# Moving the modulation pieces between the stages of a two-block transformer, and one wait of TensorE ahead of the value stage

## The chip, the cores and the metric

The kernel runs on one core of one Trainium2 chip. The metric is the device time of one execution in microseconds (us); lower is better. Engines are named as in the profile: PE is TensorE (PEld its weight loads), DVE is VectorE, ACT is ScalarE, POOL is GpSimd and SP is SyncE, whose queue issues the weight stream.

## The reference

One sequence of 256 positions and 1024 features goes through two blocks of two layers each, in float32. The first block has attention of several kinds, cross attention to a memory, and a gated feed-forward part with a short convolution. The second block is modulated by a condition vector:

```
def ada_params(cond, w, b):
    return jnp.split(jax.nn.silu(cond) @ w + b, 6, axis=-1)
...
    for i in range(DEPTH):
        sh1, sc1, g1, sh2, sc2, g2 = [t[:, None, :] for t in ada_params(c, ada_w[i], ada_b[i])]
        ax = modulate(rms_norm_2(hx, norm_mix[i]), sh1, sc1)
        ...
        hx = hx + g1 * yx
        fx = modulate(rms_norm_2(hx, norm_ffn[i]), sh2, sc2)
        hx = hx + g2 * swiglu(fx, ffn_w1[i], ffn_w3[i], ffn_w2[i])
```

`yx` is the retention mixer's output in layer 0 and the convolution mixer's in layer 1. A context sequence enters layer 0 with its own shift and scale, from `ada_params(c_ctx, ...)`. `ada_params` needs the 1024 x 6144 matrix `ada_w` of each layer: 48 pieces of 128 output columns a layer, 96 in all. The condition is one vector, so each piece is a matrix-vector product. They don't depend on the activations, so they can be done anywhere ahead of their use.

## The kernel before

**Stages and the stream.** `STAGES` lists 26 stages in the order in which they run: name, layer, number of weight pieces, and how many modulation pieces ("ada") go with each step. A step is two weight pieces. For layer 0 and 1 of the first block the stages are `qkv` (11 steps), `mkv` (2), `out` (4), `mq` (1), `mo` (1), `up` (22) and `down` (11); then come the stages of the second block: `rq`, `rg`, `rk`, `rv`, `ro` (queries, gates, keys, values, output of the retention mixer), `f13` and `f2` (feed-forward), `cx`, `cb`, `co` (convolution mixer), `f13` and `f2`. Every piece, of either kind, is 128x1024 float32 (512 KB) and comes from one tensor, `stream_d`, in the order in which it is consumed. `stage_table` works out the places. Stages named in `INTO_X` carry no modulation piece in their last step.

**Ring.** SP copies piece after piece into `ring`, eight slots. Piece r is asked for once the counter `consumed` has reached r-7, and the counter `loaded` is raised for a piece when the piece five places later has been asked for. So a late consumer holds up later loads.

**A weight piece.** ACT copies it to `WH` (rounded to fp32r, L471), DVE makes the remainder `WL` = piece - `WH` (L981, raises `consumed`), and PE does 24 matmuls with it: 16 with `WH` (against the high and low half of the activations), then 8 with `WL`. `WH` and `WL` have two slots, so ACT and DVE prepare the piece after the next while PE works.

**A modulation piece** (`ada_piece`, L990 to L999) costs PE and ACT nothing: DVE multiplies the piece with the broadcast condition `crow` and accumulates the row sums into a column of `mod` (L998). For the first 16 of the 96 a second such instruction with `crow_ctx` fills `modc` (L996). In a step with one modulation piece DVE does it after the second `WL`, ahead of the stage's own extra work (`aside`). In the last step of a stage outside `INTO_X` it comes first. Step 0 of a stage that follows a "raw" norm has an order of its own (`late`): `WL`, both evacuations, `WL`, modulation piece.

**The qkv stage.** DVE evacuates each product into `P` with the row norm (`mixed`, L1323 and L1326) and raises `bank_free`; PE waits for that count before it writes the bank again. After steps 2 to 10 `aside(step)` follows, with the rotary turns (`sine` L1236, `turned_by` L1243), the memory norm (`memory_scaled`, L1120) and, at the end of `aside(4)`, `prod` (L1275), for which PE waits in `gate_sums`. POOL does `compressed_rows` (L1600, four instructions a call) and `cosine` (L1609) beside it.

**Modulations.** `modulations(part)` adds the bias to its part of `mod` (L1379) and makes the gains `gs` (L1389), one chained DVE instruction each. Part 0 stands at the start of the second block, part 1 after the value stage, part 2 ahead of the residual at the end of `f2` (its argument `ahead`). ACT waits for `mod_ready` in `raw_norm`.

**The value stage.** PE accumulates in `accs`. After piece 2 `ret_scores(0)` writes the banks `proj`, which ACT frees when it has evacuated the last keys (L910).

Of the kernel before, what the change touches and what calls it, by code (L numbers as in the profile page):

```python
# [9 lines left out]
KB = D // 128  # L10
# [23 lines left out]

STAGES = [("qkv", 0, 2 * MIX, 0), ("mkv", 0, 4, 1), ("out", 0, 8, 1), ("mq", 0, 2, 0), ("mo", 0, 2, 0),
          ("up", 0, 2 * FB, 0), ("down", 0, FB, 1),
          ("qkv", 1, 2 * MIX, 0), ("mkv", 1, 4, 1), ("out", 1, 8, 1), ("mq", 1, 2, 0), ("mo", 1, 2, 0),
          ("up", 1, 2 * FB, 0), ("down", 1, FB, 2),
          ("rq", 0, 8, 0), ("rg", 0, 16, 0), ("rk", 0, 8, 1), ("rv", 0, 16, 2), ("ro", 0, 16, 2),
          ("f13", 0, 2 * FB, 1), ("f2", 0, FB, 0),  # L40
          ("cx", 1, 16, 0), ("cb", 1, 8, 0), ("co", 1, 8, 0), ("f13", 1, 2 * FB, 0), ("f2", 1, FB, 0)]
INTO_X = ("out", "mo", "down", "ro", "f2", "co")
N_MOD = 48
# [159 lines left out]
def transformer(nc, xT_d, memT_d, ctxT_d, cond_d, stream_d, vecs_d, const_d, rope1_d, rope2_d, decay_d,  # L203
# [5 lines left out]
    with ctx:  # L209
# [190 lines left out]
        def mod_of(layer, c):  # L400
            return mod[:, 48 * layer + KB * c:48 * layer + KB * c + KB]
# [62 lines left out]
        def _(act):  # L464
# [370 lines left out]
            def second_ffn(k, layer):  # L835

                def swiglu(step, s):
                    if s == 0:
                        if is_first(step):
                            act.preload_act_table(ACT.Silu)  # L840
                        act.wait_ge(bank_free[0], step + (n["q"] + 2))
                        A(cv[:, 0, :], cv[:, 0, :], ACT.Silu, bias=cvs[:, 0, S:S + 1]).then_inc(silu_ready, 1)  # L842
                    else:
                        upper(step, step + (n["pair"] + 1))
                weights(k, swiglu, peel=2, late=raw_root)
                n["pair"] += FB
                if layer == 0:
                    raw_norm(k + 1, gs[:, 2, :], 0, 1, shift=mod_of(1, 0), ready=3)
                else:
                    weights(k + 1, tail=squares(1))  # L850
                    n["x"] += 8
# [93 lines left out]
            def last_head(step):  # L945
                if step == 0:
                    ret_root(RET_HEADS - 1)
                if step == 1:
                    ret_high(RET_HEADS - 1)
            raw_norm(K + 4, gs[:, 1, :], 0, 1, shift=mod_of(0, 3), ready=2, after=last_head)  # L950
            second_ffn(K + 5, 0)

            def conv_in(i, s):
# [20 lines left out]
        def _(dve):  # L974
# [42 lines left out]
            def weights(k, evac=None, per=0, peel=False, before=None, gate=None, into_x=False, after=None, raw=None, ahead=None, late=None):  # L1017
# [3 lines left out]
                def part(i, last):  # L1021
# [33 lines left out]
                    for s in range(2):  # L1055
# [6 lines left out]
                        if late and evac and s == 1 and type(i) is int and i == 1:  # L1062
                            split(next_piece(st, i, s), st["p0"] + 5, s)
                            evac(1, 0)
                            dve.wait_ge(mm_done, st["p0"] + 4)
                            before(i, s)
                            evac(1, 1)
                            if st["ada"]:
                                ada(0)
                            continue  # L1070
                        if before:
                            dve.wait_ge(mm_done, i * 2 + (st["p0"] + s + 1))
# [304 lines left out]
            def biased(j0, j1):  # L1377

                chain.link(V.tensor_tensor(mod[:, j0:j1], mod[:, j0:j1], vecs[:, V_ADAB + j0:V_ADAB + j1], ALU.add))  # L1379

            def modulations(part):

                dve.wait_ge(consumed, TABLE[K + (0, 4, 7)[part]]["r0"])
                biased((0, 16, 48)[part], (16, 48, 96)[part])
                scales = [[(0, mod_of(0, 1), V_MIX2), (4, modc[:, 8:16], V_MIX2)],
                          [(1, mod_of(0, 4), V_FFN2)],
                          [(2, mod_of(1, 1), V_MIX2 + KB), (3, mod_of(1, 4), V_FFN2 + KB)]][part]
                for c, scale, gain in scales:
                    chain.link(V.scalar_tensor_tensor(out=gs[:, c, :], in0=scale, scalar=1.0, in1=vecs[:, gain:gain + KB],  # L1389
                                                      op0=ALU.add, op1=ALU.mult))  # L1390
                dve.sem_inc(mod_ready, 1)
# [15 lines left out]
            def second_ffn(k, layer):  # L1407
# [15 lines left out]
                n["pair"] += FB  # L1423
                n["silu"] += FB
                if layer == 0:
                    weights(k + 1, gate=mod_of(layer, 5), into_x=True, raw=(gs[:, 2, :], 0, mod_of(1, 0)), ahead=lambda: modulations(2))
                else:
                    weights(k + 1, gate=mod_of(layer, 5), into_x=True)

# [95 lines left out]
                if part == 1 and h:  # L1525
                    ret_low(h - 1)
            weights(K + 3, heads, before=values, after=lambda step: None)
            modulations(1)

            def last_head(step):  # L1530
                if step == 0:
# [126 lines left out]
        def _(pe):  # L1658
# [449 lines left out]

            def ret_scores(h):
                if h == 0:  # L2110
                    for s in range(2):
                        pe.wait_ge(bank_free[s], n["q"] + 1)
                    pe.wait_ge(rope_done, 4 * DEPTH + 8)
                else:
                    pe.wait_ge(ret_w, 2 * h)
                if h >= 2:
                    pe.wait_ge(ret_rms, h - 1)
                for jt in range(4):
                    for c in range(2):
                        ins = mm(proj[jt // 2][:, jt % 2 * S:jt % 2 * S + S], K2[:, 2 * h + c, 128 * jt:128 * jt + 128], Q2[:, 2 * h + c, :],  # L2120
                                 c == 0 and jt % 2 == 0, c == 1)
                ins.then_inc(ret_sc, 1)
# [17 lines left out]
                ins.then_inc(ret_ms, 1)  # L2140

            st = TABLE[K + 3]
            for p in range(16):
                h, part = divmod(p, 4)
                s = p % 2
# [146 lines left out]
```

## Time and profile before

| | |
|---|---|
| median of 3 runs | 1614.93 us (1614.89 to 1616.33) |
| profiled execution | 1614.93 us; span of its trace 1613.2 us |
| PE busy | 1573.2 us, 98% of the span |
| DVE busy | 1161.8 us, 72% |
| ACT busy | 818.5 us, 51% |
| POOL busy | 86.1 us, 5% |
| data read | 291.4 MB, 181 GB/s over the span |

A busy PE is one that has a matmul under way; matmuls are pipelined. Times in rows are microseconds from the start of the span.

### The profile page before, as it was taken

What the parts mean: (1) busy time and instruction counts of PE and PEld (TensorE: products, weight loads), DVE (VectorE), ACT (ScalarE), POOL (GpSimd) and SP (SyncE); (2) the same over time, 40 slices, a digit from 0 to 9 for tenths busy, and PEclk for the clock granted to TensorE, in tenths of its full rate; (3) what the DMA queues carried; (4) which work ended last, traced back from release to release, by engine and by line L of the source; (5) the groups of instructions that cost most, each with busy time, mean ns of one, the idle gap of its engine ahead of it and who ended that gap; (6) DMA issues with size and microseconds to landing.
All of it is one profiled execution on the core that took longest, in us unless ns stands there. A gap on an engine that the chain in (4) does not pass through costs nothing. (4 is left out here: it accounts for less than half of the span.)

```text
span 1613.2 us, 35961 instructions
## 1 busy us (share of the span) xinstructions
PE 1573.2 (98%) x12298; PEld 1463.1 (91%) x12298; DVE 1161.8 (72%) x1781; ACT 818.5 (51%) x1343; POOL 86.1 (5%) x91
## 2 busy tenths in 40 slices
PE   8999899999999989999999999999999999999998
PEld 7977789999997869999989888889999999999997
DVE  5884789988877478998867445568988468677644
ACT  5555666653556576664555212235555355555533
POOL 2100001110300001110000100000000000000000
PEclk9999999999999999999999999999999999999999
DMA  9530435458743235557945543358888545455551
GB/s 361 190 132 14 157 131 173 176 187 275 270 146 131 77 133 181 172 180 272 340 128 186 164 137 128 133 190 297 272 277 276 199 163 184 162 185 181 183 182 50
DMA packets 84234, 297.45 MB, mean 184 GB/s; under 512 B 9664, under 2 KB 12480, under 8 KB 83392
## 3 DMA queue, kind: packets, MB, share of 16 engines
q1 hardware_dynamic: 78912, 283.24, 51.0%
q10 hardware_dynamic: 5248, 13.18, 2.4%
q8 instruction: 52, 0.85, 0.2%
q14 instruction: 22, 0.18, 0.0%
HBM read 291.40 MB, written 1.05 MB: 181 GB/s over the span
## 5 line engine op out<-in xcount | busy, mean ns | idle before, releaser
L981 DVE TENSOR_TENSOR WL<-ring,WH 128x1024 fp32r<-128x1024 f32 x427 | 524.7, 1230 | 260.3 <-ACT WH L471 259.0
L471 ACT ACTIVATE WH<-ring 128x1024 fp32r (+1 forms) x419 | 441.6, 1057 | 517.8 <-PE projs L1663 249.0
L1663 PE MATMUL projs<-AH,WH 128*128 128x256 f32 (+2 forms) x2120 | 538.1, 291 | 8.9 <-ACT WH L471 4.1
L1663 PE MATMUL projs<-AL,WH 128*128 128x256 f32 (+2 forms) x2120 | 530.9, 287 | 0.3
L1663 PEld LDWEIGHTS projs<-AH,WH 128*128 128x128 f32 x2120 | 399.2, 189 | 23.7 <-DVE mk L1346 7.7
L1663 PEld LDWEIGHTS projs<-AL,WH 128*128 128x128 f32 x2120 | 401.2, 190 | 5.3 <-DVE AL L1141 1.7
L1663 PE MATMUL projs<-AH,WL 128*128 128x256 f32 (+2 forms) x2192 | 315.2, 285 | 0.2 <-DVE WL L981 0.2
L1663 PEld LDWEIGHTS projs<-AH,WL 128*128 128x128 f32 x2192 | 285.2, 189 | 7.5 <-DVE WL L981 2.5
L1663 PE MATMUL accs<-FH,WH 128*128 (+1 forms) x768 | 190.5, 284 | 2.0 <-ACT WH L471 2.0
L1663 PE MATMUL accs<-FL,WH 128*128 (+1 forms) x768 | 189.7, 281 | 0.0
L1663 PEld LDWEIGHTS accs<-FH,WH 128*128 128x128 f32 x768 | 144.3, 188 | 3.3 <-issue 3.3
L1663 PEld LDWEIGHTS accs<-FL,WH 128*128 128x128 f32 x768 | 144.8, 189 | 0.0
L998 DVE SCALAR_TENSOR_TENSOR ring<-ring,crow 128x1024 f32 (+1 forms) x96 | 118.3, 1232 | 2.9 <-DVE G L1489 0.7
L1663 PE MATMUL accs<-FH,WL 128*128 (+1 forms) x768 | 113.4, 282 | 0.0
L814 ACT ACTIVATE cv<-mk,vecs 128x256 f32<-128x256 f32 x88 | 53.1, 603 | 97.7 <-DVE mk L1346 97.7
L1663 PEld LDWEIGHTS accs<-FH,WL 128*128 128x128 f32 x768 | 101.1, 188 | 0.0
L1663 PE MATMUL accs<-AH,WH 128*128 128x256 f32 (+2 forms) x272 | 68.5, 286 | 3.4 <-DVE AL L1197 1.9
L1663 PE MATMUL accs<-AL,WH 128*128 128x256 f32 (+2 forms) x272 | 67.2, 281 | 0.0
L1355 DVE SCALAR_TENSOR_TENSOR cv<-mk,vecs,cv 128x254 f32<-128x254 f32 x88 | 53.6, 609 | 11.5 <-DVE cv L1353 0.3
L1663 PEld LDWEIGHTS accs<-AH,WH 128*128 128x128 f32 x272 | 51.2, 188 | 6.5 <-DVE AL L1197 3.1
L1638 POOL TENSOR_TENSOR FL<-prod,FH 128x256 f32 x44 | 36.2, 824 | 364.8 <-ACT FH L535 364.8
L1663 PE MATMUL accs<-WH,AH 128*128 128x512 f32 x128 | 51.7, 404 | 0.0
(261 smaller groups left out, 1867.2 us busy)
## 6 DMA issues: line engine op xcount, KB each, us to landing
ring<-in_stream SPq DMA_DIRECT2D x532, 512.0 KB, 3.8
W1v<-in_w ACTq DMA_DIRECT2D x2, 1024.0 KB, 7.2
W1k<-in_w ACTq DMA_DIRECT2D x2, 1024.0 KB, 10.3
D<-in_decay ACTq DMA_DIRECT2D x4, 512.0 KB, 5.0
x<-in_xT SPq DMA_DIRECT2D x2, 512.0 KB, 5.3
memT<-in_memT SPq DMA_DIRECT2D x1, 1024.0 KB, 11.3
mq<-P ACTq DMA_DIRECT2D x8, 128.0 KB, 5.9
ctxT<-in_ctxT ACTq DMA_DIRECT2D x1, 1024.0 KB, 8.1
```

The source lines that it names most:

```text
L471: A(WH[:, s, :], ring[:, r % RING, :], ACT.Copy).then_inc(wh_ready, 1)
L814: A(cv[:, s, :], us[:, s, :], ACT.Identity, bias=cb, scale=w2).then_inc(tap_ready, 1)
L981: V.tensor_tensor(WL[:, s, :], ring[:, r % RING, :], WH[:, s, :].bitcast(F32), ALU.subtract).then_inc(consumed, 1)
L998: V.scalar_tensor_tensor(out=piece, in0=piece, scalar=1.0, in1=crow[:], op0=ALU.mult, op1=ALU.mult, accum_out=mod[:, bass.ds(j, 1)]).then_ ...
L1355: V.scalar_tensor_tensor(out=cv[:, s, 2:S], in0=us[:, s, 0:S - 2], scalar=vecs[:, bass.ds(j + cw, 1)], in1=cv[:, s, 2:S], op0=ALU.mult, op ...
L1638: G.tensor_tensor(FL[:, bass.ds(step, 1), :].squeeze(1), prod[:], FH[:, bass.ds(step, 1), :].squeeze(1).bitcast(F32), ALU.subtract).then_i ...
L1663: return T.matmul(out, lhsT, rhs, start=start, stop=stop, skip_group_check=True)
```

## The change

The modulation pieces are handed out differently over the stages; their sum stays 96. `qkv` of layer 1 gets 1 a step (11 pieces, was 0), `out` of layer 1 gets 0 (was 3), `rk` gets 2 a step (8, was 4), `f13` of the second block's layer 0 gets 0 (was 22), its `f2` gets 1 a step (10, was 0). After the change all 48 pieces of layer 0 are done ahead of the second block, so `modulations` has two parts in place of three. And the wait for the two `proj` banks moves from `ret_scores(0)` to the head of the value stage.

```
 STAGES = [
...
-          ("qkv", 1, 2 * MIX, 0), ("mkv", 1, 4, 1), ("out", 1, 8, 1), ("mq", 1, 2, 0), ("mo", 1, 2, 0),
+          ("qkv", 1, 2 * MIX, 1), ("mkv", 1, 4, 1), ("out", 1, 8, 0), ("mq", 1, 2, 0), ("mo", 1, 2, 0),
           ("up", 1, 2 * FB, 0), ("down", 1, FB, 2),
-          ("rq", 0, 8, 0), ("rg", 0, 16, 0), ("rk", 0, 8, 1), ("rv", 0, 16, 2), ("ro", 0, 16, 2),
-          ("f13", 0, 2 * FB, 1), ("f2", 0, FB, 0),
+          ("rq", 0, 8, 0), ("rg", 0, 16, 0), ("rk", 0, 8, 2), ("rv", 0, 16, 2), ("ro", 0, 16, 2),
+          ("f13", 0, 2 * FB, 0), ("f2", 0, FB, 1),
...
-                    raw_norm(k + 1, gs[:, 2, :], 0, 1, shift=mod_of(1, 0), ready=3)
+                    raw_norm(k + 1, gs[:, 2, :], 0, 1, shift=mod_of(1, 0), ready=2)
...
-            raw_norm(K + 4, gs[:, 1, :], 0, 1, shift=mod_of(0, 3), ready=2, after=last_head)
+            raw_norm(K + 4, gs[:, 1, :], 0, 1, shift=mod_of(0, 3), after=last_head)
...
                             evac(1, 1)
-                            if st["ada"]:
-                                ada(0)
                             continue
...
-            def modulations(part):
-
-                dve.wait_ge(consumed, TABLE[K + (0, 4, 7)[part]]["r0"])
-                biased((0, 16, 48)[part], (16, 48, 96)[part])
-                scales = [[(0, mod_of(0, 1), V_MIX2), (4, modc[:, 8:16], V_MIX2)],
-                          [(1, mod_of(0, 4), V_FFN2)],
-                          [(2, mod_of(1, 1), V_MIX2 + KB), (3, mod_of(1, 4), V_FFN2 + KB)]][part]
+            def modulations(layer):
+
+                dve.wait_ge(consumed, TABLE[K + (0, 7)[layer]]["r0"])
+                biased(48 * layer, 48 * layer + 48)
+                scales = [(2 * layer, mod_of(layer, 1), V_MIX2 + KB * layer), (2 * layer + 1, mod_of(layer, 4), V_FFN2 + KB * layer)]
+                if layer == 0:
+                    scales.append((4, modc[:, 8:16], V_MIX2))
                 for c, scale, gain in scales:
...
-                    weights(k + 1, gate=mod_of(layer, 5), into_x=True, raw=(gs[:, 2, :], 0, mod_of(1, 0)), ahead=lambda: modulations(2))
+                    weights(k + 1, gate=mod_of(layer, 5), into_x=True, raw=(gs[:, 2, :], 0, mod_of(1, 0)), ahead=lambda: modulations(1))
...
             weights(K + 3, heads, before=values, after=lambda step: None)
-            modulations(1)
...
             def ret_scores(h):
                 if h == 0:
-                    for s in range(2):
-                        pe.wait_ge(bank_free[s], n["q"] + 1)
                     pe.wait_ge(rope_done, 4 * DEPTH + 8)
...
             st = TABLE[K + 3]
+            for s in range(2):
+                pe.wait_ge(bank_free[s], n["q"] + 1)
             for p in range(16):
```

## Rows read from the trace of the kernel before

**Rows 1.** Windows: busy of PE, PEld, DVE, ACT, POOL (count), clock, DMA, GB/s.
```profile
420.00:430.00 10.00, 10.00 (x87) 10.00 (x86) 7.25 (x9) 3.77 (x4) 4.61 (x4) 1.00 0.96 371
```
**Rows 2.** Chain of work that ended last: start, length, what.
```profile
1247.19 63.61 PE accs L1663 x528
...
1414.10 0.02 ACT rms L577
...
1536.98 63.59 PE accs L1663 x528
```
**Rows 3.** Timeline of ACT at the start of f13, layer 0.
```profile
1124.01 0.47 ACT L577 ACTIVATE rms<-ob,const 128x256 f32<-128x256 f32 x1 [0.79 <-PE ob L1663]
```
**Rows 4.** Who waited for whom, PE, 415 to 500 us: total, times, longest.
```profile
PE ob L1663 <- DVE prod L1275: 0.7, 1, 0.7
```
**Rows 5.** The ring with crow, ns min/median/max; then rows_v.
```profile
L998 DVE SCALAR_TENSOR_TENSOR ring<-ring,crow x96: 1215/1220/2317, 98.4 to 1245.8; 128x1024 f32 x55, 128x1024 f32<-128x1024 f32 x41
...
L1600 POOL TENSOR_TENSOR rows_v<-P,vecs x8: 710/1154/1643, 23.4 to 424.3; 64x240 f32<-64x240 f32 x8
```
**Rows 6.** Timeline around the longest modulation piece, POOL and DVE.
```profile
938.22 2.30 POOL L1646 TENSOR_TENSOR K<-K,rope 128x512 f32<-128x512 f32 x1 [8.96 <-DMA mq<-K]
939.29 2.32 DVE L998 SCALAR_TENSOR_TENSOR ring<-ring,crow 128x1024 f32<-128x1024 f32 x1
```
**Rows 7.** Timeline of POOL, DVE and ACT, steps 0 and 1 of qkv, layer 1.
```profile
420.35 4.68 POOL L1600 TENSOR_TENSOR rows_v<-P,vecs 64x240 f32<-64x240 f32 x4 [70.83 <-DVE P L1326]
421.32 0.42 DVE L1326 TENSOR_TENSOR P<-accs,rstd 128x256 f32<-128x256 f32 x1
422.01 1.75 DVE L981 TENSOR_TENSOR WL<-ring,WH 128x1024 fp32r<-128x1024 f32 x1 [0.28 <-ACT WH L471]
423.75 1.06 ACT L471 ACTIVATE WH<-ring 128x1024 fp32r<-128x1024 f32 x1 [1.77 <-PE accs L1663]
426.58 1.06 ACT L471 ACTIVATE WH<-ring 128x1024 fp32r<-128x1024 f32 x1 [1.77 <-PE projs L1663]
```
**Rows 8.** Timeline of DVE and POOL, steps 3 to 5 of that stage.
```profile
438.22 4.29 POOL L1600 TENSOR_TENSOR rows_k<-P,vecs 64x240 f32<-64x240 f32 x4 [2.50 <-DVE P L1243]
440.75 0.43 DVE L1326 TENSOR_TENSOR P<-projs,rstd 128x256 f32<-128x256 f32 x1 [0.27 <-PE projs L1663]
441.84 1.75 DVE L981 TENSOR_TENSOR WL<-ring,WH 128x1024 fp32r<-128x1024 f32 x1 [0.67 <-ACT WH L471]
442.59 3.86 POOL L1609 TENSOR_TENSOR P<-P,rope 128x512 f32<-128x512 f32 x2
447.83 0.42 DVE L1275 TENSOR_TENSOR prod<-ob,rstd 128x256 f32<-128x256 f32 x1
```
**Rows 9.** Timeline where keys end and values begin, ACT and PE.
```profile
932.33 0.58 ACT L910 ACTIVATE K<-projs 128x512 f32<-128x512 f32 x1
931.17 0.39 PE L1663 MATMUL accs<-WH,AH 128*128 128x512 f32 x1
```
**Rows 10.** Timeline at the ends of out and mo, layer 1.
```profile
568.99 0.59 PE L1663 MATMUL ob<-still 128*128 128x512 bf16 x2
576.88 1.75 DVE L1114 RECIPROCAL rstd<-rms 128x256 f32<-128x256 f32 x1 [1.75 <-ACT rms L577]
599.16 0.59 PE L1663 MATMUL ob<-still 128*128 128x512 bf16 x2
606.43 1.75 DVE L1114 RECIPROCAL rstd<-rms 128x256 f32<-128x256 f32 x1 [1.14 <-ACT rms L577]
```
**Rows 11.** Timeline of DVE at the start of the second block.
```profile
803.84 0.17 DVE L1389 SCALAR_TENSOR_TENSOR gs<-mod,vecs 128x8 f32<-128x8 f32 x1
804.04 0.17 DVE L1389 SCALAR_TENSOR_TENSOR gs<-modc,vecs 128x8 f32<-128x8 f32 x1
```
**Rows 12.** Timeline of DVE at the end of f2, layer 0.
```profile
1307.55 0.21 DVE L1379 TENSOR_TENSOR mod<-mod,vecs 128x48 f32<-128x48 f32 x1
1308.67 3.23 DVE L1012 SCALAR_TENSOR_TENSOR x<-accs,mod,x 128x256 f32<-128x256 f32 x8 [0.50 <-PE accs L1663]
```

## The prediction

> **What bounds the kernel now.** I read the page's busy times, then the chain that ended last, the waits of PE, and the timelines of the stages that the change touches. PE has 1573 of 1613 us busy, so only two things cost time: work that PE has to do, and moments at which PE stands still. The change gives PE no work and takes none away. A modulation piece is DVE work of 1.22 us [rows 5] (1.15 from one start to the next), and it matters only where DVE already sets PE's pace. So I ask of each stage whether DVE is late there.
>
> PE needs 2.83 us for a weight piece in qkv: ACT, which waits for the end of each, starts at 423.75 and at 426.58 and takes 1.06 us [rows 7]. Then comes DVE's `WL` (1.15), so DVE is ready some 2.3 us after a piece ended. PE wants that `WL` one piece and 16 of 24 matmuls later, 2.83 + 1.9 = 4.7 us after. DVE may be about 2.4 us late before PE notices. One extra piece of 1.15 us is hidden in a plain step; it shows where DVE has much else to do.
>
> **f13, layer 0: 22 pieces leave.** The row norm's root starts at 1124.01 [rows 3] and PE gets to f2 at 1247.19: 123.18 us. The same stage of layer 1, with no modulation piece, takes 1536.98 - 1414.10 = 122.88 us [rows 2]. So 22 pieces, 25 us of DVE work, cost PE 0.30 us today. Gain: 0.3.
>
> **f2, layer 0: 10 pieces come.** Both f2 stages run 63.6 us [rows 2] and the steps have room (2 x 1.15 + 1.15 of 5.76 us). What changes is the end. Today DVE begins `modulations` at 1307.55, and after it still waits 0.50 us for PE before the residual at 1308.67 [rows 12]. Afterwards the last modulation piece fills 1307.5 to 1308.65, and `modulations` follows it (0.25 for the bias add, 0.20 for each of two `gs`, from start to start as in [rows 11]): the residual starts 0.65 to 0.7 us late. Behind it are queued the low halves, for which PE waits. Loss: 0.7.
>
> **qkv, layer 1, step 0.** Here the piece is number 15 of the first 16, so it is two chained instructions. DVE would start them at 421.35, where it now evacuates step 1 [rows 7]. POOL runs its four `rows_v` instructions then, 0.71 us each when undisturbed [rows 5]. How do the two get along? A POOL instruction that runs from 938.22 to 940.5 and a modulation piece that starts at 939.29 meet: the piece takes 2.32 us and not the median 1.22 [rows 5, 6], that is, 1.1 from POOL's end on. The `WL` at 422.01 takes 1.75 us in the middle of `rows_v` [rows 7]. So I take it that each of the two waits until the other's instruction has ended. (The Trainium skill, SBUF — State Buffer, section "SBUF: two separate sides", says the same: the port pair is an exclusive lock, held for the whole instruction, against a DVE instruction with two SBUF inputs. By that rule, the trace agrees: the 2.32 us. If instead the two only ran side by side, this term would be near zero and the next 1.3.)
> Alternating: first instruction 421.99 to 423.15, POOL to 423.9, second to 425.1, POOL to 425.8 (meanwhile the evacuation from `accs`, which isn't held up in rows 7), `WL` of step 2 from 425.8 to 427.0. PE starts step 2 at 423.75, where ACT was released [rows 7], and wants that `WL` at 425.65. Loss 1.4; without the collisions DVE would have it at 425.35: 0. From above: both instructions at 2.32 us give 427.9 or so, 2.3. I take 1.4.
>
> **qkv, steps 3 and 4.** `prod` at 447.83 [rows 8] is already what PE waits for (0.7 us [rows 4]). Ahead of it DVE gets one modulation piece in step 3 and one in step 4, 2.3 us; its idle time on the way is 0.27 + 0.67 us [rows 8], which leaves 1.3 to 1.4. But POOL's six instructions (`rows_k`, two `cosine`) start when `turned_by(0)` is done, so they shift back by 1.1 too, and their end at 442.59 + 3.86 = 446.45 [rows 8] moves past DVE's `sine(2)`. In the same alternation, times without the 1.4 of before: the piece of step 4 waits for the third `rows_k` (0.7), `turned_by(1)` for the fourth (0.6), `sine(2)` for a `cosine` (1.2), and `memory_scaled`, which runs free today, for the last `cosine` (1.2). `prod` is evacuated at about 450.8: late by 3.0. Ends: 1.3 and 3.5, the latter with one more short collision. I take 2.9, near the upper end, because today's `WL` at 441.84 shows this very alternation (1.75 us in the middle of `rows_k` [rows 8]).
>
> **qkv, end.** The piece of step 10 comes ahead of the evacuation that frees the bank for mkv. Following the steps with 1.15 more each, DVE catches up by step 9 (PE has 7 us of side work in steps 5 to 9), then `aside(9)` and two pieces in a row delay the evacuation of step 10 to 0.2 to 0.3 us after PE wants the bank. Loss 0.3 (0 to 0.5). Cover that may go: the stream now asks for three pieces a step while W1 and the swaps load, and the DMA share is already 0.96 from 420 to 430 us, at the full clock of 1.00 [rows 1]. The ring has five to six pieces in hand, about 10 us; I cost it at 0, bound 2.
>
> **mkv, layer 1.** The two-instruction piece is gone there, 1.2 us of DVE; what follows waits for ACT and PE. 0.
>
> **out, layer 1: 3 pieces leave.** From PE's first warm-up matmul to the reciprocal of the norm it is 576.88 - 568.99 = 7.89 us at the end of out, with a modulation piece in front, and 606.43 - 599.16 = 7.27 at the end of mo, without [rows 10]. Same norm, same shapes. Gain: 0.6.
>
> **Start of the second block.** `modulations` has one more chained instruction (0.20 from start to start) and a wider bias add, in front of the `gs` and the root on which everything waits [rows 11]. Loss: 0.2. The part that stood after rv, 0.4 us of DVE, was hidden; 0. The dropped `ready=2` waits for something long past; 0.
>
> **rk: 4 more pieces.** A keys piece has matmuls of 512 columns and keeps PE nearly twice 2.83 us, in which DVE has one `WL`, one modulation piece (2.3 us together) and part of a turn. 0.
>
> **The moved wait.** Today PE begins the values at 931.17, and ACT frees the second key bank at 932.33 + 0.58 = 932.91 [rows 9]; nobody minds, since the scores come only after the third piece. Afterwards PE stands until 932.95 or so before its first matmul. Behind it is all of rv, and the list of PE's waits from 930 to 1118 us is empty, so nothing takes it up. Loss: 1.8 (1.6 to 1.9).
>
> **Sum.** -0.3 + 0.7 + 1.4 + 2.9 + 0.3 - 0.6 + 0.2 + 1.8 = +6.4 us. The profiled execution's own time was 1614.93 (span 1613.2 and 1.7 around it), which is also the median, so 1621.3 us, 0.4% slower. All bounds at their low end: -0.3 + 0.6 + 0 + 1.3 + 0 - 0.6 + 0.2 + 1.6 = +2.8, 1617.7. All at the high end: -0.3 + 0.7 + 2.3 + 3.5 + 0.5 - 0.6 + 0.2 + 1.9 + 2 = +10.2, 1625.1.
>
> **Rivals.**
> *Collisions with POOL don't add up.* The qkv stage loses just its 1.3 to 1.6. For it: of 96 modulation pieces the median took 1.22 us [rows 5]. Against it: the long `WL`s [rows 7, 8]. With 0 and 1.4 for the two terms the sum is +3.5, 1618.4: at the edge of what can be told. Chance 0.2.
> *The stream falls behind in qkv.* Three pieces a step, 277 GB/s, plus 2 MB of W1 against some 400 GB/s; ACT would wait for `loaded`. It needs 1.4 MB to queue up in the 10 us that the ring covers. Against it: down of layer 0 runs at three pieces a step, and PE waits for ACT once there, 1.0 us. 2 MB at 400 GB/s are 5 us of stream; if half of that reaches PE, the total is +9, 1624, and all of it gives 1626.5. Chance 0.1.
> *Faster: f13 gives more than 0.3.* If PE in f13 were held back in every step by DVE, 22 steps would have to give 0.45 us each to outweigh 6.7 us of losses and reach 0.2%. Place: the steady steps; deciding point 0.45 us a step. Against it: 0.3 us over the stage [rows 2, 3]. 1611.7 at that point. Chance 0.03.
> *The moved wait is free*, if PE stood anyway for `WH` of the first values. Against it: PE starts at 931.17 [rows 9]. Then 1619.5. Chance 0.07.
> The forecast itself: 0.6.
>
> **Chances.** 0.2% is 3.2 us, about what a measurement of this kernel can tell from no change. Slower by more: the forecast, the stream, the free wait, and two fifths of the first rival (the rest of it within), 0.85; within: 0.12; faster: 0.03. The range runs from the first rival's low edge to short of the second's.
>
> **What would show it.** In the profile after: PE waits on DVE's `WL` near 425 us (1.4), and on `prod` (3 to 4 us in place of 0.7); modulation pieces of over 2 us in qkv; a hole of 1.8 us ahead of the first values; 122.9 us for f13; the residual of f2 without a wait for PE. I am wrong if PE's wait for `prod` stays under 2 us or ACT waits for the stream in qkv.

## The result, and the profile after

| | before | after |
|---|---|---|
| median, same chip | 1615.08 us (1614.89 to 1616.33) | 1626.86 us (1625.55 to 1627.89) |
| profiled execution | 1614.93 us, span 1613.2 | 1627.96 us, span 1626.3 |
| DVE busy | 1161.8 us | 1166.5 us |

The ratio is 1.0076, with a 95% interval from 1.0063 to 1.0088. The change costs 11.8 us in the medians and 13.0 us between the two profiled executions. The forecast was +6.4 us, so the sign was right and the size was about half of what came. The range was to end short of the stream rival's 1624 us, and even the sum of all upper bounds, 1625.1 us, lies below the measured time. Lines of the kernel after stand two or three lower than before in places: `prod` is L1273, `mixed` L1321 and L1324, `mk` of the up stage L1344, PE's matmul helper L1660.

First, who PE waited for in the qkv and mkv stages (415 to 500 us; total, times, longest):

```profile
PE ob L1660 <- DVE prod L1273: 2.8, 1, 2.8
PE projs L1660 <- DVE WL L981: 0.9, 1, 0.9
PE projs L1660 <- DVE P L1324: 0.5, 1, 0.5
PE accs L1660 <- ACT WH L471: 0.2, 1, 0.2
```

The wait for `prod` has grown from 0.7 us [rows 4] to 2.8. The other two new waits are those forecast near 425 us (0.9 for `WL`, where 1.4 stood) and at the end of the stage. The forecast had put the wait for `prod` at 3 to 4 us. The timeline of steps 0 and 1, DVE, POOL and ACT:

```profile
420.25 6.64 POOL L1597 TENSOR_TENSOR rows_v<-P,vecs 64x240 f32<-64x240 f32 x4 [70.84 <-DVE P L1324]
421.21 1.75 DVE L996 SCALAR_TENSOR_TENSOR cprod<-ring,crow_ctx 128x1024 f32<-128x1024 f32 x1
...
423.01 1.62 DVE L998 SCALAR_TENSOR_TENSOR ring<-ring,crow 128x1024 f32<-128x1024 f32 x1
...
424.90 1.41 DVE L981 TENSOR_TENSOR WL<-ring,WH 128x1024 fp32r<-128x1024 f32 x1
...
427.62 1.07 ACT L471 ACTIVATE WH<-ring 128x1024 fp32r<-128x1024 f32 x1 [2.92 <-PE projs L1660]
```

POOL's four `rows_v` take 6.64 us beside the two products, where they took 4.68 [rows 7]; the products take 1.75 and 1.62 us and not 1.22 [rows 5]. The `WH` that marks the end of a PE piece comes at 427.62, 1.04 later than at 426.58 [rows 7]. Steps 3 to 5, and the work after `prod`:

```profile
440.40 5.29 POOL L1597 TENSOR_TENSOR rows_k<-P,vecs 64x240 f32<-64x240 f32 x4 [3.40 <-DVE P L1241]
...
445.04 1.74 DVE L998 SCALAR_TENSOR_TENSOR ring<-ring,crow 128x1024 f32<-128x1024 f32 x1
445.77 3.83 POOL L1606 TENSOR_TENSOR P<-P,rope 128x512 f32<-128x512 f32 x2
...
446.71 1.76 DVE L1241 TENSOR_TENSOR P<-P,cv 128x512 f32<-128x512 f32 x1
448.51 1.65 DVE L1234 TENSOR_TENSOR cv<-swapped,rope 128x512 f32<-128x512 f32 x1
...
450.99 0.42 DVE L1273 TENSOR_TENSOR prod<-ob,rstd 128x256 f32<-128x256 f32 x1
...
455.57 0.28 ACT L739 ACTIVATE csum<-accs 128x128 f32<-128x128 f32 x1 [2.81 <-PE accs L1660]
```

`prod` comes 3.2 us later than at 447.83 [rows 8], after three DVE instructions in a row that take longer beside POOL. Two of the three did so in the kernel before as well:

```profile
443.52 1.78 DVE L1243 TENSOR_TENSOR P<-P,cv 128x512 f32<-128x512 f32 x1
445.33 1.67 DVE L1236 TENSOR_TENSOR cv<-swapped,rope 128x512 f32<-128x512 f32 x1
```

New is the modulation piece ahead of them, at 1.74 us. But the partial sums, evacuated as `csum`, are late by still more: 4.58 us after `prod` began, where the kernel before needed 3.10 (447.83 to 450.93). The windows say why (busy of PE, PEld, DVE, ACT, POOL, then the granted clock, DMA share, GB/s):

```profile
420.00:430.00 10.00, 9.12 (x77) 8.91 (x76) 9.97 (x14) 3.19 (x3) 6.57 (x4) 1.00 0.98 392
430.00:440.00 10.00, 10.00 (x87) 10.00 (x86) 8.40 (x14) 4.24 (x4) 3.21 (x2) 1.00 1.01 386
450.00:460.00 10.00, 8.54 (x170) 8.39 (x171) 8.37 (x16) 3.17 (x6) 0.00 (x0) 0.83 0.48 168
```

and the last of these windows in the kernel before:

```profile
450.00:460.00 10.00, 10.00 (x140) 9.73 (x130) 7.51 (x14) 5.36 (x10) 0.00 (x0) 1.00 0.47 160
```

From 450 to 460 us the granted clock is 0.83: after its wait PE spent part of the stretch at the lower of its two levels (1.2 and 2.4 GHz). DMA is full from 420 to 440, yet ACT never waits for the stream there.

The largest part lies where nothing was changed, in `up` of layer 1. DVE in the kernel before, from one loop pass to the next:

```profile
679.88 0.42 DVE L1346 TENSOR_TENSOR mk<-projs,rstd 128x256 f32<-128x256 f32 x1
...
685.41 0.43 DVE L1362 TENSOR_TENSOR prod<-cv 128x256 f32<-128x256 f32 x1 [0.21 <-DVE cv L1355]
685.81 0.42 DVE L1346 TENSOR_TENSOR mk<-projs,rstd 128x256 f32<-128x256 f32 x1
```

and in the kernel after:

```profile
682.21 0.42 DVE L1344 TENSOR_TENSOR mk<-projs,rstd 128x256 f32<-128x256 f32 x1 [0.19 <-issue]
...
687.75 0.43 DVE L1360 TENSOR_TENSOR prod<-cv 128x256 f32<-128x256 f32 x1 [0.21 <-DVE cv L1353]
688.36 0.42 DVE L1344 TENSOR_TENSOR mk<-projs,rstd 128x256 f32<-128x256 f32 x1 [0.19 <-issue]
```

The same instructions take 5.93 us a pass before and 6.15 after. The 0.22 us are a gap ahead of the pass's first instruction that no wait explains ("issue"). From the first to the last of ACT's 22 L821, one a step, it is 123.72 and 127.94 us.

The moved wait, at the start of the values:

```profile
942.98 0.58 ACT L910 ACTIVATE K<-projs 128x512 f32<-128x512 f32 x1
...
943.66 0.47 PE L1660 MATMUL accs<-WH,AH 128*128 128x512 f32 x1 [1.68 <-issue]
```

PE now begins after ACT's last keys and not 1.2 us ahead of them [rows 9]. Then f13 of layer 0: the norm's root, and from the chain the last of f13 and the first of f2:

```profile
1136.47 0.48 ACT L577 ACTIVATE rms<-ob,const 128x256 f32<-128x256 f32 x1 [0.79 <-PE ob L1660]
...
1144.16 115.20 PE projs L1660 x960
1259.36 57.62 PE accs L1660 x480
```

That is 122.89 us, where it was 123.18. And the end of f2, layer 0:

```profile
1319.62 1.22 DVE L998 SCALAR_TENSOR_TENSOR ring<-ring,crow 128x1024 f32 x1
...
1321.65 2.44 DVE L1012 SCALAR_TENSOR_TENSOR x<-accs,mod,x 128x256 f32<-128x256 f32 x6 [0.16 <-PE accs L1660]
```

This view ends inside the residual, so it shows six of its eight instructions. The residual starts 12.98 us later than before [rows 12], but the matmuls of the last piece ahead of it only 12.18 (1307.67 and 1319.85): it is DVE that is late now, by 0.8 us, and the 0.16 us put down to PE are no wait for it.

All of it, stage by stage, from the times of ACT's instructions at the borders (after minus before):

| stretch | us | forecast |
|---|---|---|
| up to qkv, layer 1 | -0.1 | 0 |
| qkv and mkv, `prod` to `csum` at its old 3.10 us | +4.0 | +4.6 |
| the 1.48 us more between `prod` and `csum` | +1.5 | none |
| attention of layer 1 | +1.2 | none |
| out | -0.6 | -0.6 |
| up | +4.2 | none |
| start of the second block | +0.2 | +0.2 |
| rq, rg, rk | +0.2 | 0 |
| start of the values | +1.9 | +1.8 |
| f13, layer 0 | -0.3 | -0.3 |
| f2, layer 0 | +0.8 | +0.7 |
| sum | +13.0 | +6.4 |

### The profile page after: what moved, and what is told of

It reads as the page before. It is cut to its first block, busy times and chain, and to the rows that moved or that the text cites. A ratio compares the mean times of both kernels' runs of the same rounds, so it can differ in the third digit from the quotient of the medians.

```text
span 1626.3 us, 35908 instructions
## 1 busy us (share of the span) xinstructions
PE 1576.1 (97%) x12283; PEld 1466.4 (90%) x12298; DVE 1166.5 (72%) x1780; ACT 816.6 (50%) x1343; POOL 87.6 (5%) x91
## 4 chain that ended last, share of the span: by engine, by line
PE 72%; DVE 14%; ACT 7%; issue 5%; DVEq 1%; ACTq 1%; DMA 0%; SPq 0%; POOL 0%
PE projs L1660 34%; PE accs L1660 32%; PE ob L1660 5%; DVE WL L981 4%; ACT WH L471 3%; DVE mk L1344 2%; DVE cv L1353 2%; DVE cv L1351 1%; ACT FH L535 1%; DVE rstd L1112 1%; ACT AH L562 1%; PE projs L1906 1%; ACT scr L641 1%; DVE ring L998 1%; DVE prod L1360 0%
## 5 line engine op out<-in xcount | busy, mean ns | idle before, releaser
L1660 PE MATMUL projs<-AH,WH 128*128 128x256 f32 (+2 forms) x2120 | 538.5, 291 | 12.5 <-ACT WH L471 4.3
L1660 PE MATMUL projs<-AL,WH 128*128 128x256 f32 (+2 forms) x2120 | 530.9, 287 | 0.3
L1660 PEld LDWEIGHTS projs<-AH,WH 128*128 128x128 f32 x2120 | 399.5, 189 | 28.9 <-DVE mk L1344 14.0
L1660 PEld LDWEIGHTS projs<-AL,WH 128*128 128x128 f32 x2120 | 401.1, 189 | 5.5 <-DVE AL L1139 1.7
L1660 PE MATMUL projs<-AH,WL 128*128 128x256 f32 (+2 forms) x2192 | 315.3, 286 | 1.2 <-DVE WL L981 1.2
L1660 PEld LDWEIGHTS projs<-AH,WL 128*128 128x128 f32 x2192 | 285.2, 189 | 8.7 <-DVE WL L981 4.1
L1660 PE MATMUL accs<-FH,WH 128*128 (+1 forms) x768 | 190.4, 284 | 2.0 <-ACT WH L471 2.0
L1660 PE MATMUL accs<-FL,WH 128*128 (+1 forms) x768 | 189.6, 281 | 0.0
L1660 PEld LDWEIGHTS accs<-FH,WH 128*128 128x128 f32 x768 | 144.3, 188 | 3.3 <-issue 3.3
L1660 PEld LDWEIGHTS accs<-FL,WH 128*128 128x128 f32 x768 | 144.8, 189 | 0.0
L998 DVE SCALAR_TENSOR_TENSOR ring<-ring,crow 128x1024 f32<-128x1024 f32 (+1 forms) x96 | 120.3, 1253 | 2.8 <-DVE G L1487 0.7
L1660 PE MATMUL accs<-FH,WL 128*128 (+1 forms) x768 | 113.4, 282 | 0.0
L1660 PEld LDWEIGHTS accs<-FH,WL 128*128 128x128 f32 x768 | 101.0, 188 | 0.0
L1660 PE MATMUL accs<-AH,WH 128*128 128x256 f32 (+2 forms) x272 | 68.6, 286 | 3.4 <-DVE AL L1195 1.9
L1660 PE MATMUL accs<-AL,WH 128*128 128x256 f32 (+2 forms) x272 | 67.2, 281 | 0.0
L1660 PEld LDWEIGHTS accs<-AH,WH 128*128 128x128 f32 x272 | 51.2, 188 | 6.4 <-DVE AL L1195 3.1
L1660 PE MATMUL accs<-WH,AH 128*128 128x512 f32 x128 | 51.8, 405 | 1.7 <-issue 1.7
```

What stands on the lines that cost most here:

```text
L998: V.scalar_tensor_tensor(out=piece, in0=piece, scalar=1.0, in1=crow[:], op0=ALU.mult, op1=ALU.mult, accum_out=mod[:, bass.ds(j, 1)]).then_ ...
L1660: return T.matmul(out, lhsT, rhs, start=start, stop=stop, skip_group_check=True)
```

## The experiments

All are timed beside the kernel before on the same chip. "Prod" is when `prod` starts, counted from the root of the qkv norm of layer 1 (ACT's L577, 416.09 before and 415.98 after): 31.74 us before, 35.01 after. "Mkv end" is ACT's last `Vm` of that layer on the same scale: 80.98 and 86.48.

### The place of the up loop in VectorE's program

Five runs here, and two further down, move DVE's loops by instructions that do nothing. A wait on a semaphore long complete is put ahead of the memory attention, where DVE has time; the compiler joins two such waits into one instruction.

```diff
                 weights(k0 + 3, before=cross_q, late=root)
                 n["q"] += 1
+                for _ in range((a, b)[i]):
+                    dve.wait_ge(setup_v, 3)
                 attend(units_memory())
```

`(a, b)` are the waits in layer 0 and in layer 1. The first two runs have them in layer 1 alone, 33 in the kernel before (17 instructions) and 30 in the kernel after (15). The next three are the kernel before with (16, 38), (32, 32) and (64, 64).

> The kernel before, with 33 waits on a semaphore that is long complete, put on VectorE just ahead of the memory attention of layer 1; they become 17 instructions, so that VectorE's up loop of layer 1 stands at the place in its program that it has in the changed kernel. All computation is the same. Theory (the loop's place in the program sets what its jump back costs): the period of a step of that loop goes from 5.93 to 6.15 us and the time rises by about 4.4 us, to some 1619. Rival (the loop was slowed by its state on entry, its ring slots or the traffic, not by its place): the period stays 5.93 us and the time is within 1 us of the kernel before.

Measured: 1615.44 us against 1614.89, ratio 1.0004 (0.9994 to 1.0013). The step stays at 5.93 us. This went against the theory, in the form in which it stood.

> The changed kernel, with 30 such waits at the same place, 15 instructions, so that the up loop of layer 1 stands 32 instructions behind its place in the kernel before. Theory that place counts, with a period of 32 instructions or a divisor of it: the step goes back from 6.15 to 5.93 us and the time falls by 4.4 us to about 1622.5. If place counts with a longer period: the step has some third length between 5.9 and 6.2 us. Rival (not the place): 6.15 us stays, time within 1 us of the changed kernel.

Measured: 1624.41 us, ratio 1.0059 (1.0043 to 1.0076). The step is 6.03 us, between the two. The identical loop, in an otherwise identical kernel, goes 0.12 us faster a pass for 15 idle instructions that run once. And the gap has moved to another place of the pass, ahead of the second convolution instruction:

```profile
680.91 0.48 DVE L1354 SCALAR_TENSOR_TENSOR cv<-mk,vecs,cv 128x255 f32<-128x255 f32 x1
681.66 0.61 DVE L1356 SCALAR_TENSOR_TENSOR cv<-mk,vecs,cv 128x254 f32<-128x254 f32 x1 [0.27 <-DVE cv L1354]
...
684.28 0.49 DVE L1356 SCALAR_TENSOR_TENSOR cv<-mk,vecs,cv 128x254 f32<-128x254 f32 x1
```

So the place does count, and the first run had the wrong one. The trace shows what its count had left out: each modulation piece is two instructions on the chip, the product and a read of its sum.

```profile
445.04 1.74 DVE L998 SCALAR_TENSOR_TENSOR ring<-ring,crow 128x1024 f32<-128x1024 f32 x1
446.71 0.08 DVE L998 DVE_READ_ACCUMULATOR ring<-ring,crow 128x1 f32 x1
```

The qkv stage is written out step by step, so its 11 pieces, one of them double, put 12 such reads ahead of the loop, and less is left in mkv and out: 10 net, and the shift is 27, not 17. The instructions in the traces give the same: from the root to the loop the kernel after executes 298 on DVE and the kernel before 283, and of `out`'s loop, which is passed three times, a pass has 8 and 14. With each pass beyond the first taken off, 282 and 255 are left.

> The kernel before, with waits on a long complete semaphore on VectorE ahead of both memory attentions: 8 instructions in layer 0 and 19 in layer 1. The up loop of layer 1 then stands 27 instructions behind its place in the kernel before, which is its shift in the changed kernel too once the reads of the accumulator are counted (17 instructions of the program and some 10 such reads; the 17 of the first padded run left those out). Theory (place): layer 1's step is 6.15 us, up by 0.22, as in the changed kernel, so +4.4 us there; layer 0's step, now 8 instructions further, leaves 6.03 or not, by at most 0.1 to 0.2 us either way (2 to 4 us in all). Rival (not the place but what the changed kernel did ahead of the loop): layer 1 stays at 5.93 us.

Measured: 1619.97 us against 1614.93, ratio 1.0030 (1.0019 to 1.0042). Layer 1's step is 6.15 us, and the unexplained gap is there, in a kernel that has no part of the change:

```profile
681.78 0.42 DVE L1364 TENSOR_TENSOR prod<-cv 128x256 f32<-128x256 f32 x1 [0.21 <-DVE cv L1357]
682.40 0.42 DVE L1348 TENSOR_TENSOR mk<-projs,rstd 128x256 f32<-128x256 f32 x1 [0.19 <-issue]
```

Layer 0, moved by 8, stays at 6.03. That shows the place as the cause of the 4.2 us, and it was got by moving nothing else. Why a place costs time isn't shown.

> The same with 16 instructions in each layer: the up loop of layer 0 moves by 16 and that of layer 1 by 32. Theory that the cost goes by the place modulo 32 or a divisor: layer 1 stays at 5.93 us; if the period is 16, layer 0 stays at 6.03 too and the time is that of the kernel before plus at most 1 us; if it is 32, layer 0's step changes, by up to 0.2 us (4 us in all). Rival (only the absolute distance counts): layer 1's step changes too.

Measured: 1615.53 us, ratio 1.0003 (0.9993 to 1.0013). Layer 0 at +16 goes down to 5.91 us a step, layer 1 at +32 goes up to 6.04: no period of 16 or 32. The two cancel in the total, which alone would have read "no effect".

> As the run with 16 and 32 instructions of shift, with 32 and 64. If the cost of a place repeats every 64 instructions, layer 1's step is 5.93 us as in the kernel before; layer 0's, at +32, can't be told from the others. Rival (no such period, the shift counts in another unit than the program's instructions): another length between 5.90 and 6.15 us.

Measured: 1613.81 us, ratio 0.9992 (0.9982 to 1.0001). Layer 1 at +64 is at 5.93 again, layer 0 at +32 at 5.91. A period of 64 fits; one point doesn't prove it. Every run of this study, layer 1:

| shift | 0 | 17 | 25 | 27 | 32 | 42 | 64 |
|---|---|---|---|---|---|---|---|
| step, us | 5.93 | 5.93 | 5.90 | 6.15 | 6.04 | 6.03 | 5.93 |
| runs | before | 1 | 4 | 4 | 1 | 2 | 1 |

At 25 stand the two runs below that leave out a double or two single pieces, the one that puts the pieces behind, and the last run of this document; at 27 the kernel after, its two versions with only PE edits, and the padded kernel before.

### The qkv stage and TensorE's clock

Filler ahead of the gate sums, layer 1 only, in the kernel after:

```diff
                     if step == 5:
+                        if i == 1:
+                            turn_over(10, acc[1])
                         gate_sums()
```

> The changed kernel, with 10 matmuls 128x512 on zeros into a free bank ahead of the gate sums of qkv step 5 in layer 1 (about 2.1 us at 213 ns each, inside TensorE's wait of 2.8 us for prod). Theory (that wait lets TensorE's clock fall, and the narrow partial sums then run at the lower level): the granted clock of 450:460 goes from 0.83 to about 1.00, the stretch from the gates' exponential to the partial sums' eviction from 3.02 to about 1.0 us, and the time falls by about 2 us to 1625. Rival (the stretch is long for a data wait or for the count of columns): clock or not, it stays near 3 us and the time stays within 0.5 us, or rises by what of the filler isn't covered.

Measured: 1624.22 us, ratio 1.0054 (1.0037 to 1.0071). The window:

```profile
450.00:460.00 10.00, 9.31 (x188) 8.62 (x187) 9.26 (x16) 3.24 (x7) 0.00 (x0) 1.00 0.49 161
```

`prod` is as late as before (35.02), `csum` follows 3.09 us after it, mkv ends at 84.99 and not 86.48. The clock was the whole of the 1.5 us in that execution. Against this stands the padded kernel after, which has no filler and the same wait of 2.8 us, but a clock of 1.00. So I set all runs side by side:

| kernel | PE's wait for `prod` | clock 450:460 | `prod` to `csum` |
|---|---|---|---|
| before; five padded ones; after, pieces of steps 3 and 4 left out | 0.7 to 0.8 | 1.00 | 3.08 to 3.10 |
| after | 2.8 | 0.83 | 4.58 |
| after, 15 padded | 2.8 | 1.00 | 3.09 |
| after, wait back | 2.8 | 0.66 | 5.17 |
| after, piece of step 0 left out | 3.4 | 0.66 | 5.16 |
| after, filler (two kernels) | 0.7 | 1.00 | 3.09 |
| after, pieces behind | 1.3 | 1.00 | 3.08 |

A long wait makes the fall possible, not sure: it came in three profiled executions of four, with two sizes, and in none of the ten with a wait of 1.3 us or less. (The Trainium skill, TensorE: Matmul & The Clock Gate, section "HAM oscillation — how this bites in real kernels", has long waits of TensorE lower its clock for the matmuls behind them. The traces agree in kind: 0.83 and 0.66 behind waits of 2.8 and 3.4 us, though one wait of 2.8 us left it at 1.00.) All recorded executions point the same way, if by little: the mean granted clock over the whole kernel is 0.9952 to 0.9958 in the four kernels with the long wait, and 0.9965 to 0.9978 in the others. The kernel before took 1613.4 us in its executions at 0.999 and 1616.2 in those at 0.996, so between it (0.9975) and the kernel after (0.9958) the clock makes an estimated 1.6 us. The same view settles the 1.2 us of layer 1's attention, which the change doesn't touch. From ACT's last `WH` of mkv to its first of out it is 53.16 or 53.17 us in four profiles (before, and three changed kernels), all with 1.00 from 530 to 550 us; it is 54.28 to 54.36 in the ten others, all with a clock under 1 in that stretch (0.83 in 540:550 of the kernel after). Padded kernels before have it as well. So it goes with the execution and not with the change, and the profiled execution of before was one of the four. What lowers the clock there wasn't tried.

Two pieces left out of the kernel after, with their columns zeroed, so that the result of this kernel lacks them:

```diff
+                if leave_out:
+                    if ctx_too:
+                        chain.link(V.memset(modc[:, j:j + 1], 0.0))
+                    V.memset(mod[:, j:j + 1], 0.0).then_inc(consumed, 1)
+                    return
...
-                        ada_piece(ada_place(st, i, a, last), j, j < 16 if type(j) is int else st["j0"] < 16, last)
+                        ada_piece(ada_place(st, i, a, last), j, j < 16 if type(j) is int else st["j0"] < 16, last,
+                                  st["name"] == "qkv" and i in (3, 4))
```

> The changed kernel, whose modulation pieces of qkv steps 3 and 4 in layer 1 are left out: their two columns are set to zero in place of the products, their data is still loaded. Theory (these two pieces make prod late, 3.27 us with the step 0 share of 1.15): prod comes some 2.1 us earlier after the start of the stage, at about 32.9 us, TensorE's wait for it is 0.7 us and not 2.8, the granted clock of 450:460 is 1.00, and the memory stage ends 2.1 + 1.5 us earlier. Rival (the wait comes from the rotation's slow neighbours on GpSimd, or from the whole backlog since step 0): prod earlier by less than 1 us.

Measured: 1619.40 us, ratio 1.0025 (1.0016 to 1.0035). `prod` at 32.90 us, 2.1 earlier; wait 0.7; clock 1.00; mkv ends at 82.86, 3.6 earlier. As the theory had it. (The up loop, at +25, went down to 5.90 us too, which is why the total fell by more.)

The same with `i in (0,)`:

> The changed kernel, whose modulation piece of qkv step 0 in layer 1, with its context product, is left out in the same way. Theory (with both at 1.75 and 1.62 us beside GpSimd's compression rows they hold up the second lower half WL and with it the second step): the fifth of TensorE's pieces ends 1.15 us earlier, as in the kernel before (10.49 us after the stage's start, not 11.64), and the rest of the stage follows by as much, less what the waits of steps 3 and 4 take up. Rival (the 1.15 us are made up by the wait at prod anyway): the step is earlier, but prod is not.

Measured: 1621.88 us, ratio 1.0044 (1.0030 to 1.0058). The fifth piece is at 10.49 us, exactly as in the kernel before, so step 0's piece costs the stage 1.15 us at that point. But `prod` moves from 35.01 to 34.38 only, and PE waits 3.4 us for it:

```profile
PE ob L1666 <- DVE prod L1279: 3.4, 1, 3.4
PE projs L1666 <- DVE P L1330: 0.5, 1, 0.5
```

The rival is right in part: without step 0's piece `prod` is late by 2.6 (34.38 - 31.74), without those of steps 3 and 4 by 1.2 (32.90 - 31.74), with all of them by 3.3. They don't add up in full. The timelines between the pieces of steps 2 and 3 show where the half microsecond is. In this run POOL starts its `cosine` just ahead of a `WL`, which takes 2.32 us:

```profile
434.26 1.29 POOL L1612 TENSOR_TENSOR P<-P,rope 128x512 f32<-128x512 f32 x1 [0.61 <-DMA mq<-P]
434.31 2.32 DVE L981 TENSOR_TENSOR WL<-ring,WH 128x1024 fp32r<-128x1024 f32 x1
```

In the kernel after the `WL` comes first and takes 1.22:

```profile
434.63 1.22 DVE L981 TENSOR_TENSOR WL<-ring,WH 128x1024 fp32r<-128x1024 f32 x1
434.83 2.17 POOL L1606 TENSOR_TENSOR P<-P,rope 128x512 f32<-128x512 f32 x1 [3.64 <-DMA mq<-P]
```

From there on DVE is 0.6 us apart in the two runs, as `prod` is, and not 1.15.

Then the order of DVE's work in a step:

```diff
+                behind = st["name"] == "qkv" and st["ada"] == 1
...
-                        if st["ada"]:
+                        if st["ada"] and not behind:
                             ada(0)
...
-                        if not last and s >= 2 - st["ada"]:
+                        if not last and s >= 2 - st["ada"] and not behind:
                             ada(s - (2 - st["ada"]))
...
                         part(i, i + 1 == st["steps"])
                         after(i)
+                        if behind and i + 1 < st["steps"]:
+                            piece(i, 0, False)
```

> The changed kernel, with each modulation piece of qkv in layer 1 put behind the work of its step (rotation, scaling of the memory, gate product) on VectorE instead of ahead of it. Theory (prod waits because two pieces stand ahead of it in VectorE's order): the piece of step 4 is out of prod's way and that of step 0 comes a little later; prod comes 1.2 to 1.8 us earlier than in the changed kernel (35.0 us after the stage's start), TensorE's wait for it falls from 2.8 to 1.0-1.6 us, and the memory stage ends as much earlier, more if the clock stays at 1.00. Rival (the delay is only handed to the next step's lower halves): the end of the memory stage is within 0.5 us of the changed kernel at the same clock.

Measured: 1619.30 us, ratio 1.0029 (1.0020 to 1.0039). `prod` at 33.43, 1.6 us earlier; PE waits 1.3 us for it; mkv ends at 83.57. That is 1.4 us before the kernel with filler, which had the same clock of 1.00, and 2.9 before the kernel after.

```profile
PE ob L1667 <- DVE prod L1280: 1.3, 1, 1.3
...
PE projs L1667 <- DVE WL L981: 0.9, 1, 0.9
PE projs L1667 <- DVE P L1331: 0.7, 1, 0.7
```

All 96 pieces are done, in the same steps. The two orders differ by 7.6 us in their medians, taken in different sets of runs; the up loop, shifted to +25 by this edit, has 4.5 of it (127.94 and 123.39 us from the first to the last L821), the qkv stage 2.9.

### The moved wait, and three causes at once

The wait for the banks back in `ret_scores(0)`, in the kernel after:

```diff
             def ret_scores(h):
                 if h == 0:
+                    for s in range(2):
+                        pe.wait_ge(bank_free[s], n["q"] + 1)
                     pe.wait_ge(rope_done, 4 * DEPTH + 8)
...
-            for s in range(2):
-                pe.wait_ge(bank_free[s], n["q"] + 1)
             for p in range(16):
```

> The changed kernel, with the wait for the free banks ahead of the first retention scores again and not ahead of the first values. Theory (it costs the 1.81 us that the traces show between the last key and the ro norm): the time falls by 1.8 us to about 1625.0. Rival (the retention loop has slack of its own, so that it was something else in that stretch): within 0.5 us of the changed kernel.

Measured: 1625.47 us, ratio 1.0061 (1.0044 to 1.0078). From the last keys' evacuation to ACT's first `WH` of the values it is 4.63 us, as in the kernel before, against 6.52 in the kernel after: 1.89 us. In the medians, of different sets of runs, 1.4 of them show.

> The changed kernel with three of the causes taken back at once: the filler ahead of the gate sums, the wait for the free banks at its old place, and VectorE's 15 instructions ahead of layer 1's up loop (6.03 us a step). Theory (they add): 2.6 us from the loop, 1.9 us from the wait and the clock's 1.5 us in the profiled stretch, so about 1621 us; what is left over the kernel before is 4.0 us in the qkv and memory stages, 2.0 in the loop. Rival (they overlap or bring new waits): 1622.5 or more.

Measured: 1621.26 us, ratio 1.0042 (1.0027 to 1.0058), where 1621 was expected. The filler, the old wait and the 15 instructions add: clock 1.00, step 6.03 us, 84.97 at the end of mkv.

### Both up loops at faster places

> The kernel before, with waits on a long complete semaphore on VectorE ahead of the memory attentions: 16 instructions in layer 0 and 9 in layer 1, so that the up loop of layer 0 stands 16 and that of layer 1 25 instructions further. Theory (place): layer 0's step is 5.91 us as it was at +16 (6.03 before; 21 steps between the first and the last mark, so -2.3 us), layer 1's is about 5.90, as in the runs that left pieces out, which stood 2 accumulator reads ahead of the changed kernel's +27 (5.93 before; -0.6 us); together some 1612 us, 0.2% faster than the kernel before. Rival (the shift has to be right to the instruction, and mine is counted from the program, not from the chip's code): layer 1 at 5.93 to 6.15 us, time between 1612.5 and 1617.

Measured: 1613.44 us against 1614.90, ratio 0.9991 (0.9982 to 1.0000). It is the kernel before with 16 and 9 idle instructions, (32, 18) waits. Both loops went as forecast, 5.91 and 5.90 us a step, and the time didn't: it was put at 1612. In the profile the two loops give back 2.2 and 0.3 us. Of that 1.5 shows in the median: 0.1% faster than the kernel before, at the edge of what can be told, and 0.8% faster than the kernel after. It keeps the old places of the modulation pieces; none of the runs says that the new ones are worth having.

## Why the prediction was wrong

**The step that failed** is the rule on which the whole sum was built: "I ask of each stage whether DVE is late there", asked only of stages that get or lose a piece, so that an untouched one costs nothing. A loop of DVE that PE hangs on here also paid for where its instructions lie in the program. That was 4.2 us in `up`, shown by the padded kernels: the kernel before with the loop moved by the same 27 instructions has the 6.15 us step and takes 1620.0 us. Against that one the kernel after stands 6.9 us higher in the medians of different sets of runs (as ratios, 1.0076 less 1.0030 is 7.4 us, give or take some 2.7). The forecast of 6.4 was for that difference, without knowing it; that it comes so near is luck in part, since the 7 us hold a cost of the clock that the sum didn't have. No bound of the range held such a term, and none of the rivals did.

**The clock** was taken as full ("at the full clock of 1.00 [rows 1]"), though the sum itself let PE wait 3 to 4 us for `prod`. What follows such a wait ran at a lower clock in three profiled executions of four: 1.5 us in that of the kernel after, 0 to 2.1 in others.

**qkv, step 0**: forecast 1.4, measured 1.15 at step 0. The alternation with POOL was right in kind. The pieces took 1.75 and 1.62 us beside `rows_v`, each about half a microsecond more than alone; none was over 2 us, as I had said some would be.

**qkv, steps 3 and 4**: forecast 2.9 above that, measured 2.1 (35.01 against 32.90 without these two pieces). What was wrong is the last of the four collisions that I counted: `memory_scaled` was put at 1.2 and wasn't held up (0.88 us for two, as before). The other three came, at 0.5 for the piece of step 4, 1.1 for `turned_by(1)` and 1.0 for `sine(2)` above their undisturbed 1.22 and 0.69 us, where 0.7, 0.6 and 1.2 stood. Against that, DVE made up only half of its idle 0.27 + 0.67 us: 0.42 are still there, ahead of the `WL` in front of the piece. The bounds of 1.3 and 3.5 held.

**qkv, end**: forecast 0.3 with 0.5 as its bound, measured 0.7, beyond it (from `prod` to the end of mkv 49.97 us at full clock, 49.24 before), of which PE's wait for the evacuation L1324 is 0.5.

**The stream**: cost 0, measured 0. ACT waited for no piece from 415 to 500 us, though DMA stood at 0.98 to 1.01 for 20 us. The rival that put 0.1 on it had nothing; that its 1626.5 us lie next to the measured time is chance.

**out, start of the second block, f13, f2, the moved wait**: -0.6, +0.2, -0.3, +0.7 and +1.8 forecast; -0.6, +0.2, -0.3, +0.8 and +1.9 measured. The mechanisms came as told: f13 takes 122.89 us, as its twin in layer 1 does, and the residual of f2 no longer waits for PE.

**Rivals.** "Collisions with POOL don't add up" was right in part (1.2 and 2.6 us give 3.3 and not 3.8, and one of the four collisions counted didn't come), but nowhere near the 1.4 us that it left to the two terms. "The moved wait is free" fell by 1.89 us. My own test, "I am wrong if PE's wait for `prod` stays under 2 us or ACT waits for the stream", came out in favour, and the number was still wrong: it tested the terms that I had, not whether there were others.

## What to carry to other kernels

When an edit changes how many instructions an engine's program has, compare the step time of every later loop on that engine, the untouched ones first, and pad the kernel before to the same place before you put a difference down to the edit; a gap that has grown at the same spot of each pass is the sign, whether the view marks it "issue" or puts it down to the engine's own previous instruction. Fill work belongs behind the instruction that another engine waits for, not ahead of it: the order in a step was worth 1.4 us here, the same work at the same step. And where a sum gives TensorE a wait of a few microseconds, add a term for the lower clock behind it, or fill the wait.

## What the runs showed of the hardware

- The same loop body on VectorE, 27 instructions, took 5.90, 5.93, 6.03 (6.04) or 6.15 us a pass by nothing but the number of instructions ahead of it in the program; 27 against 25 makes 0.25 us a pass. The place within the pass at which the engine idles moves with it. A shift of 64 gave the old time again. What in the chip does this was not tried.
- The read of an accumulated sum (`DVE_READ_ACCUMULATOR`) is an instruction of its own, 0.08 us of busy time, and counts in that place.
- After waits of 2.8 us, and one of 3.4, TensorE's granted clock in the next 10 us was 1.00, 0.83 or 0.66 in different executions, and the narrow partial sums that follow took 3.09, 4.58 or 5.17 us from `prod` on. With the wait filled with matmuls on zeros it was 1.00 both times.
- A product of 128x1024 on VectorE that runs against two-input work of GpSimd took 1.62 to 1.75 us and not 1.22, and four GpSimd instructions took 6.64 us and not 4.68, in the same stretch.
